# Relative-bias tables by one-hot products on TensorE, and the early projections as three rounded products with ScalarE rounding and GpSimd subtracting

## What is computed

```python
# first block, twice (DEPTH = 2)
h = layernorm(x)
proj = h @ w_in[layer]                       # -> aq ak av ag  bq bk bv bf bg  cq ck cv cg
oa = differential attention (4 heads, partial rope) * silu(ag)
ob = forgetting attention  (4 heads, cumulated log gates) * silu(bg)
oc = stick-breaking attention (4 heads) * silu(cg)
h = layernorm(ALPHA * h + concat(oa, ob, oc) @ w_out[layer])

# second block, once
h = rms_norm(x); proj = h @ w_in_2
score = sum over 8 index heads of relu(iq . ik) * iw ; sel = top_k(score, 128)
bias  = rel_bias[t5_bucket(pos[q] - pos[k])]          # 32 buckets, 4 heads
o_a = softmax(q . k_sel * scale + bias) @ v_sel       # 4 heads
o_b = gated linear recurrence in chunks of 64         # 4 heads
o_c = latent attention with its own low-rank q and kv # 4 heads
mixed = sum of sigmoid(gates) * (o @ w_up)            # three branches
x = x + mixed @ w_out_2
x = x + (silu(h @ w_gate) * (h @ w_up)) @ w_down      # h = rms_norm(x), D_FF = 2816
return rms_norm(x)
```

## Time and profile before

| | |
|---|---|
| runs, us | 2116.68, 2116.22, 2117.9; median 2116.68 |
| profiled execution: span from first to last instruction | 2112.8 us |
| median less the span | 3.9 us |
| mean granted TensorE clock | 0.942 of full speed |
| TensorE / VectorE / ScalarE / GpSimd busy | 90% / 54% / 32% / 1% |

### The profile page before, as it was taken

How to read it: one execution, slowest core, us unless ns; L and a number is a source line. 1 busy time by engine, 2 the same in 40 slices (tenths; PEclk the granted TensorE clock), 3 DMA queues, 4 the chain that set the end, 5 groups by cost and what they waited for, 6 DMA issues and landing times.

```text
span 2112.8 us, 19184 instructions
## 1 busy us (share of the span) xinstructions
PE 1902.5 (90%) x6900; PEld 1142.6 (54%) x6900; DVE 1142.6 (54%) x2306; ACT 667.5 (32%) x1340; POOL 25.4 (1%) x50
## 2 busy tenths in 40 slices
PE   5999999889899998989998876868999979999997
PEld 2444444434434444445333453556777868888785
DVE  4376676731999888532862352464445444444412
ACT  1123235311132344112112232335455334434411
POOL 2000000000000000000000000000000000000000
PEclk9999999999999998999998978978999979999998
DMA  6121112021211110032302011002333313332220
GB/s 219 40 80 40 41 49 67 27 80 40 80 40 40 40 70 1 1 111 72 89 20 60 12 59 30 14 18 75 90 90 102 113 41 99 100 98 84 98 100 40
DMA packets 153006, 135.79 MB, mean 64 GB/s; under 512 B 12673, under 2 KB 126977, under 8 KB 152913
## 3 DMA queue, kind: packets, MB, share of 16 engines
q1 hardware_dynamic: 149504, 124.53, 19.4%
q0 software_dynamic: 3408, 10.04, 1.6%
HBM read 130.36 MB, written 4.19 MB: 64 GB/s over the span
## 4 chain that ended last, share of the span: by engine, by line
PE 74%; DVE 16%; ACT 6%; issue 3%; DMA 1%; SPq 0%; DVEq 0%; ACTq 0%
PE proj L1262 24%; PE proj L1242 21%; PE proj L1259 11%; DVE rel_bias L1881 3%; PE proj L1239 2%; PE attn_out L1415 2%; PE score L1435 2%; PE score L1372 2%; PE proj L1435 1%; PE attn_out L1435 1%; PE turned_probs L1401 1%; DVE E L1951 1%; PE proj L1268 1%; PE turned_probs L1435 1%; DVE index_and_shared L1874 1%
## 5 line engine op out<-in xcount | busy, mean ns | idle before, releaser
L1262 PE MATMUL proj<-hT,weights 128*128 128x512 f32 x1216 | 561.9, 614 | 20.5 <-DVE raw L2135 11.4
L1262 PEld LDWEIGHTS proj<-hT,weights 128*128 128x128 f32 x1216 | 232.1, 196 | 302.6 <-issue 278.3
L1881 DVE SCALAR_TENSOR_TENSOR rel_bias<-index_and_shared,bias_deltas,rel_bias 128x128 f32<-128x128 f32 (+3 forms) x480 | 232.7, 547 | 4.3
L1242 PE MATMUL proj<-hT_high,weights_high 128*128 128x512 f32 x544 | 218.6, 402 | 7.6 <-DVE hT_low L2160 6.0
L1242 PE MATMUL proj<-hT_high,weights_low 128*128 128x512 f32 x544 | 215.8, 397 | 0.0
L1242 PE MATMUL proj<-hT_low,weights_high 128*128 128x512 f32 x544 | 215.5, 396 | 0.0
L2151 DVE TENSOR_TENSOR weights_low<-weights,weights_high 128x1024 fp32r<-128x1024 f32 (+1 forms) x122 | 135.3, 1116 | 96.4 <-ACT weights_high L1705 96.4
L1259 PE MATMUL proj<-weights,hT 128*128 128x512 f32 (+1 forms) x384 | 151.7, 553 | 0.1
L1705 ACT ACTIVATE weights_high<-weights 128x1024 fp32r<-128x1024 f32 (+1 forms) x122 | 111.5, 961 | 74.3 <-DMA weights<-in_w_ffn_down 60.5
L1242 PEld LDWEIGHTS proj<-hT_high,weights_high 128*128 128x128 f32 x544 | 103.2, 190 | 41.5 <-issue 9.5
L1453 ACT ACTIVATE tg<-proj 128x512 f32<-128x512 f32 x66 | 39.5, 599 | 267.0 <-PE proj L1242 212.2
(11 more groups left out here) (388 smaller groups left out, 2567.3 us busy)
## 6 DMA issues: line engine op xcount, KB each, us to landing
weights<-in_w_in SPq DMA_DIRECT2D x15, 2048.0 KB, 8.5
weights<-in_w_in SPq DMA_DIRECT2D x38, 512.0 KB, 4.2
weights<-in_w_ffn_gate SPq DMA_DIRECT2D x22, 512.0 KB, 4.1
weights<-in_w_ffn_up SPq DMA_DIRECT2D x22, 512.0 KB, 5.3
weights<-in_w_ffn_down SPq DMA_DIRECT2D x11, 1024.0 KB, 4.9
weights<-in_w_in SPq DMA_DIRECT2D x9, 1024.0 KB, 5.8
weights<-in_w_out SPq DMA_DIRECT2D x4, 2048.0 KB, 10.7
weights<-in_w_out SPq DMA_DIRECT2D x4, 1024.0 KB, 5.1
```

What stands on the lines that cost most here:

```text
L1242: mm = nc.tensor.matmul(ps[:, :], w_[:, k, c0:c0 + P], x_[:, k, :], start=first, stop=last)
L1262: mm = nc.tensor.matmul(ps[0:gr["M"], :], w[:, k, c0:c0 + gr["M"]], x[:, k, :], start=first, stop=last)
L1881: ins = nc.vector.scalar_tensor_tensor(o, mk, d, o, ALU.mult, ALU.add)
```

## The change

It does four things.

1. **Bias tables.** The 124 `bias` steps go. A small product (`bias_table`) makes, for each head, a row of 256 values indexed by 127 - residue; GpSimd stores it to DRAM and loads it back with one row shift for each partition (`circulant`). For each head a group `bias_rows` multiplies it by a one-hot matrix of the positions' residues modulo 128, and a group `bias` for each query tile multiplies the result by the keys' one-hot matrix. ScalarE copies both out. VectorE writes the two ends (keys ahead; keys 128 or more behind) over it with two `copy_predicated`. Two tables are made at each tick, in the first layer.
2. **Early projections.** All projections of stages 1 to 4, save the latents' second ones (`qb`, `kvb`), are made by three rounded products. `hT` is made as `hT_high` and `hT_low` at once by each `to_hT`; `y` is split in eight steps before `wo`.
3. **Weights.** Slabs of 128 columns (one piece of 8 x 128) for F groups and "wide" slabs of 512 columns in four pieces for T groups; a ring of 6 raw slots and one of 4 high slots in the first block, 4 and 2 in the second's woven stage, 9 and 9 in the tail. Everywhere, the tail too, ScalarE rounds and GpSimd subtracts in place. `place_splits` sets where in the list each piece's `split` stands.
4. **Order.** `wo` is done half 0 for all four tiles, then half 1 tile by tile with the layernorms; the last tile's transposes stand after the next stage's first two T groups; `wo2` has two wide slabs in place of four of 256 columns; `hi` is projected earlier.

In the diff `sp` is SyncE, `pool` GpSimd, `pe` TensorE, `act` ScalarE and `dve` VectorE.

```diff
-BIAS_RATES = {"A": 2.1, "B": 1.0, "C": 0.75}
+RAW_RING, HIGH_RING = [SLOT * i for i in range(6)], [SLOT * i for i in range(6, 10)]
+RAW_RING_2, HIGH_RING_2 = RAW_RING[0:4], [SLOT * 8, SLOT * 9]
+RAW_TAIL, HIGH_TAIL = [PIECE * i for i in range(TAIL_RING)], [PIECE * (TAIL_RING + i) for i in range(TAIL_RING)]
...
+    def slab(name, K=KD, cols=P, wide=False, split=True, **kw):
+        raws, highs = state["rings"]
+        n = 4 if wide else 1
...
+            at = state[ring]
+            if at + n > len(on):
+                at = 0
+            sl[ring] = on[at]
+            state[ring] = (at + n) % len(on)
...
-        while state["bias_due"] >= 1:
-            state["bias_due"] -= 1
-            if state["bias"] < len(bias_steps) and not only_block1:
-                steps.append(("bias", bias_steps[state["bias"]]))
+        for _ in range(2):
+            if state["bias"] < len(tables) and not only_block1:
+                h, t = tables[state["bias"]]
+                if t == 0:
+                    state["shifted"] = group("bias_rows", head=h)
+                g = group("bias", head=h, tile=t, rows=state["shifted"])
+                steps.append(("bias_ends", g))
                 state["bias"] += 1
...
+        for c in range(6):
+            steps.append(("split_x", ("y", c, 1)))
+        wo = slab("wo", wide=True, cols=512, layer=l, half=0)
...
+        wide_tiles(wo, (2, 3), dst=("resid", 0), src="y", layer=l)
+        wo = slab("wo", wide=True, cols=512, layer=l, half=1)
         for t in range(NT):
+            wide_tiles(wo, (t,), dst=("resid", 1), src="y", layer=l)
             steps.append(("ln", (l, t)))
...
+def place_splits(steps, groups, slabs, pieces):
...
+        seq = max(p["free_high"], min(p["free_raw"] + 2, slabs[p["slab"]]["first"] - 2))
+        k = max(at.get(seq, -1), start[p["after"]], before)
+        while steps[k + 1][0] not in ("group", "half", "down"):
+            k += 1
...
+            for p in pieces:
+                consumed(sp, p["free_raw"])
+                for dst, src in piece_loads(p):
+                    sp.dma_start(dst, src).then_inc(p["loaded"], 16)
...
+                elif op == "layer" and not only_block1:
+                    pool.wait_ge(table_stored, 16)
+                    pool.dma_start(circulant, table_back).then_inc(table_loaded, 16)
+                elif op == "split":
+                    p = pieces[arg]
+                    pool.wait_ge(w_high, p["nth"])
+                    nc.gpsimd.tensor_tensor(piece_view(WR, p, "raw"), piece_view(W, p, "raw"),
+                                            piece_view(WR, p, "high"), ALU.subtract).then_inc(w_low, 1)
...
+            def arrived(q):
+                    if p["split"]:
+                        pe.wait_ge(w_low, p["nth"])
...
                 elif op == "split":
+                    p = pieces[arg]
+                    act.wait_ge(p["loaded"], p["landed"])
+                    consumed(act, p["free_high"])
+                    nc.scalar.activation(piece_view(WR, p, "high"), piece_view(W, p, "raw"), ACT.Copy).then_inc(w_high, 1)
...
-                elif op == "split":
-                    i, q, n = arg["slab"], arg["piece"], arg["cols"]
-                    nc.vector.tensor_tensor(half_slots(WL, slabs[i])[:, r], half_slots(W, slabs[i])[:, r],
-                                            half_slots(WH, slabs[i])[:, r], ALU.subtract).then_inc(w_low, 1)
```

More of the change, by code:

```diff
@@ L430, in plan @@
             steps.append(("norm", dict(tile=NT - 1, nth=NT - 1)))
-        for t in ((NT - 2, NT - 1) if final_layer else (NT - 1,)):
-            for half in range(2):
-                group("to_hT", tile=t, half=half, layer=l, **(dict(norm=t) if final_layer else {}))
+            turn_rows(NT - 2, layer=l, norm=NT - 2)
     if not only_block1:
-        second(steps, groups, slabs, items, units, state, slab, group, weave, flush)
-    annotate(steps, groups, items, units)
-    return dict(steps=steps, groups=groups, slabs=slabs, items=items, units=units)
@@ L442, in second @@
+def second(steps, groups, slabs, items, units, state, slab, used, group, turn_rows, wide_tiles, weave, flush):
     l = DEPTH
@@ L444, in second @@
     steps.append(("angles", 0))
-    state["slots"] = [0, 1]
-    s_iq = slab("iq", K=KD, cols=512)
-    s_ak = slab("avak", K=KD, cols=392)
+    s_av = slab("avw", cols=136)
+    for t in range(NT):
+        if t == 2:
+            turn_rows(NT - 1, layer=DEPTH - 1, norm=NT - 1)
+        group("T", s_av, N=136, K=KD, tile=t, dst=("av", 0))
     for c in range(4):
-        group("F", s_iq, c0=128 * c, M=P, K=KD, dst=("qk", 4 + c), scale=1.0)
+        group("F", slab("iq", c0=128 * c), K=KD, dst=("qk", 4 + c), scale=1.0)
@@ new lines, in second, with values_hi, from_rest, latents_q @@
+    hold, rot = {}, {}
+    def values_hi(t):
+        if t == 0:
+            hold["hi"] = slab("hi", wide=True, cols=512)
+        group("T", hold["hi"], N=512, K=KD, tile=t, dst=("V", 512))
+    def from_rest(name, c, dst):
+        return group("F", slab(name, c0=128 * c), K=KD, dst=dst, scale=1.0)
+    def latents_q(c):
+        if c == 0:
+            state["rings"], state["raw"], state["high"] = (RAW_RING_2, HIGH_RING_2), 0, 0
+        from_rest("mq", c, ("cq", c))
+    def kpe():
+        rot["kpe"] = from_rest("mpe", 0, ("raw", 0))
@@ L557, in hgrn_gate @@
     def hgrn_gate(h):
-        g = group("gate", hold["last_hgrn"] if h < 3 else hold["hgrn"], c0=256, M=P, K=KD, chunk=4 + h, layer=l,
-                  first=False, unit=None)
+        g = group("gate", slab("hgrn", c0=HG + 128 * h), K=KD, chunk=4 + h, layer=l, first=False, unit=None)
         steps.append(("gate2", g))
@@ L616, in second @@
     steps.append(("split_x", ("mix", 7, 1)))
-    wo = tail[24:28]
-    for quarter in range(4):
-        last = quarter == 3
+    for half in range(2):
+        wo = slab("wo2", wide=True, cols=512, half=half)
+        last = half == 1
         for t in range(NT + last):
             if t < NT:
-                group("T", wo[quarter], c0=0, N=256, K=KD, tile=t, dst=("resid2", quarter), src="mix", parts=True)
-                if t in (1, 2):
-                    split_weights()
+                wide_tiles(wo, (t,), dst=("resid2", half), src="mix")
             if last:
@@ L645, in second @@
             steps.append(("split_x", ("act", c, 1)))
-        steps.append(("down", dict(i=i, slab=tail[28 + KF + i])))
-        split_weights(2)
+        two = [slab("down", K=1, cols=1024, at=2 * i + k) for k in range(2)]
+        for sl in two:
+            used(sl, len(groups) + i)
+        steps.append(("down", dict(i=i, slabs=two)))
     for t in range(NT):
```

718 lines of the change are left out of this document (359 added, 359 removed).

## The result

The changed kernel takes 2146.57 us (median of 4, 2146.41 to 2148.73); the kernel before, run beside it, 2116.52. The ratio is 1.0142, 95% interval 1.013 to 1.0154: 1.4% slower, where 2000 us and 5.5% faster were forecast. The profiled execution has a span of 2146.9 us.

What follows compares the result with a forecast made beforehand. The prediction took TensorE, busy 90% of the span, as the bound, then places where VectorE holds it up. Its terms summed to -117 us: span 2112.8 to 1996, with 3.9 us around it 2000 us; range 1945 to 2070.

Steps and rivals of the forecast that it cites:

- TensorE's gain: Projections, index phase and recurrence: 114 groups fall from 6.87 to 5.6 us as rounded products, -145 us.
- The four groups of 136 columns: Narrow groups, 7.4 us together before: 12 us as short rounded matmuls, bounds 7 to 21, so +5.
- VectorE's relief of 41 us: Both woven stages with drains: removing VectorE's bias steps gives -13 and -28 us, together -41, bounds 0 and -75.
- the drain: End of the first layer's woven stage: 12 to 14 attention items at 9 to 10 us each, -13 us.
- The tables at 12 us: First layer: four row groups of 0.86 us and 16 table groups, 8.6 us, on TensorE, +12.
- GpSimd's 2.4 us a piece: Weight slabs: a GpSimd subtraction takes 2.4 us, twice VectorE's, leaving TensorE to set the steady state.
- the coupling: GpSimd against VectorE's own steps: +5 us for an effect the trace can't show, bounds 0 and 50.
- rival 2: GpSimd and VectorE hold each other up on two-SBUF-input steps: 35 to 55 us more, 2045 us; chance 22%.
- wo to wo: Between wo's halves: the second half's slab loads late, leaving an 11 us hole in two layers, +22.
- hidden in the steady state: ScalarE's extra 115 rounded pieces, 120 us over 1440 us at a third of its load, cost nothing there.
- The recurrence: Recurrence stage: 12 of the 114 groups changing form, each falling from 6.87 to 5.6 us.
- Rival 4: Front held by chains, not TensorE: rounded products gain nothing, only the tables' relief counts, 2133 us; chance 3%.

Runs made afterwards that it cites:

- e14: The changed kernel without the table groups and without GpSimd's subtractions (third product takes the rounded weights): 2041.56 us, ratio 0.9639 to the kernel before.
- e1: The changed kernel with the 20 table groups left out and a VectorE fill of zeros for the predicated copies: 2106.57 us, ratio 0.9951 to the kernel before.
- e13: The changed kernel with VectorE's old bias steps in place of the tables, and without GpSimd's subtractions: 2086.11 us, ratio 0.985 to the kernel before.
- e15: The kernel before with the bias tables alone, fp32 projections kept and no GpSimd arithmetic: 2119.91 us, ratio 1.0017 to the kernel before.
- e5: The changed kernel with all 20 table groups in one block ahead of layer 0's first woven job: 2127.68 us, ratio 1.0054 to the kernel before.
- e3: The changed kernel with the weight subtractions on VectorE instead of GpSimd, at the same places: 2179.42 us, ratio 1.0292 to the kernel before.
- e8: The changed kernel with wo's second half multiplied by the first half's slab in both layers: 2121.47 us, ratio 1.002 to the kernel before.
- e17: The changed kernel with one wo slab for both halves, both halves of a tile multiplied one after the other: 2128.43 us, ratio 1.0051 to the kernel before.
- e18: A 2088.63 us version (GpSimd rounding narrow slabs, tables in a block, VectorE subtracting wo and av) with wo's second half one tile ahead of the layernorms: 2089.12 us.

## Why the prediction was wrong

The miss is 147 us. By medians it falls into three parts: with neither tables nor GpSimd (e14) the kernel takes 2041.6, where the sum without its 12 us for tables stood at 1988: 54 (at least, since the 1988 still hold what the sum had put down for GpSimd). GpSimd adds 2106.6 - 2041.6 = 65 (e1 against e14). The tables add 40 (the changed kernel against e1) where 12 were counted: 28.

1. **TensorE's gain: right.** The forecast was -145 + 5 - 3 = -143, the tables apart. In e14 TensorE's busy time is 1754.6 us, 148 less than before. In the tail and the woven stages a group of 24 takes about 5.5 us at full clock. The four groups of 136 columns took 21 us, the upper bound, where 12 were taken: they ran at the lower clock. The tail was right within 5 us: 7 us were gained in the feed-forward, and the stretch of wo2 came out 4 us longer where 3 less were forecast.

2. **VectorE's relief of 41 us on top of that: the first step that failed.** In layer 1's stage (F1 to L1) the sum had 29 groups x 1.27 = 37 us and 27 of relief beside them. The stage of e14 is 43 us shorter. TensorE's busy time in it fell by 44 (303.6 to 259.3), and its idle time, which the relief was to take away, stayed (15 before, 16 in e14). So the stage gained what TensorE's work and its clock (0.95 to 0.96) gave, and no more. The relief was not without worth: e14 is 44.6 us faster than e13, 34 of them in this stage. But the two gains are not separate terms. The rounded products alone (e13, without GpSimd as e14) took 9 us off the stage, the relief alone 15 (e15, which has its tables in the other layer), both together 43, and not 37 + 27. In layer 0 the 13 us of relief were put in the drain. In e15 the drain's last attention product ends 31.2 us behind L0, in the kernel before 36.2, so that some 5 of them were there. In e14 it ends 40.0 us behind L0, the gain being lost in a hole that the sum did not have (5).

3. **The tables at 12 us: the second.** I priced them as TensorE's work, which came to 16 us, and looked for no queue. Each group is read out by ScalarE and holds one of two banks, so a projection behind it waits for ScalarE's queue (the chain of the first ticks), and after the waits the products run at a lower clock (e1). Price 40 us woven, 19 less in a block (e5), and a 29 us longer stage even in the old kernel (e15). What stands queued behind a wait that the change adds was asked of the slabs, and not of the tables.

4. **GpSimd's 2.4 us a piece was right (2.5), its effect was not.** I gave the coupling 5 us and rival 2 a chance of 22%. Rival 2's mechanism is shown: VectorE's steps are lengthened by 96 us in all (858.6 against 762.2). It put 220 us there and took 16 to 25% of it as visible, 35 to 55; the lengthening was less, and the cost of GpSimd's part as a whole, duration and hold together, 65 to 71 us. How it divides between the two was not separated: e3 takes both away and puts a queue in their place.

5. **The holes: one was missing, and so was a wait.** wo to wo was forecast as 11 us a layer, which e8 bears out (11 and 15). But the list has no hole ahead of wo's first half, and there is one in each layer, 10.3 us long (7.9 in e14, where it waits for ScalarE). The load of the half's first piece is issued only when the last woven projection ends, at 393.6, and takes 3.9 us. Its rounding then stands behind six steps of splitting `y` in ScalarE's queue:

```profile
398.94 3.22 ACT hT_high L1774 x6
402.15 0.96 ACT weights_rounded L1758
403.18 2.37 POOL weights_rounded L1240
405.63 4.62 PE proj L1294 x12
```

The holes of the two layers are 20.6 of the 34.8 us that L1294 waits for GpSimd. The low halves of the turned rows were counted as VectorE's work alone; at the two boundaries TensorE waits 11.4 and 11.9 us for them, and 11.6 more for its transposes at the second, where it waited 7.5 in all for ScalarE's `hT` before. So the first boundary, L0 to F1, is 20 us longer than before: TensorE's busy time fell by 8.5 us (112.9 to 104.4, at a clock of 0.83 where it was 0.93; 12 cheaper groups were to give 15), and its idle time rose by 29. Putting groups elsewhere among the layernorms did not change that (e17, e18). The prediction called ScalarE's roundings hidden in the steady state; in the chain of the changed kernel one stands behind an item that top-k has held up, and TensorE's group behind both:

```profile
1098.57 0.76 DVE z L1990
1099.85 1.06 ACT weights_rounded L1758
1100.98 2.36 POOL weights_rounded L1240
1103.47 8.16 PE proj L1298 x24
```

6. **The recurrence** was forecast at -13 and came at -12 (latents to tail). Rival 4, that the front is held by chains, came nearest to the measured time (2133). That is luck in the number: TensorE's gain was there, and was spent again on waits that rival 4 does not name.

## What to carry to other kernels

A gain on the engine that is 95% busy and a relief of its helper are not two terms to add: in layer 1's stage one alone gave 9 us, the other alone 15, both 43, where the sum had 64. Forecast the busy engine's time with both, and ask of its idle time by itself who will still hold it up. Work moved "to the idle engine" has three prices beyond its duration: a place in the in-order queue of whoever reads it out, the bank it holds, and, between GpSimd and VectorE, the steps with two SBUF inputs. Ask of every read-out that the change adds in whose queue it stands and which bank it holds: the tables and the low halves of the turned rows cost TensorE waits of this kind. Where two changes came together, build the four combinations (here 2117, 2120, 2208 and 2147 us): the tables are worth nothing alone, and 62 us beside the rounded products.

## What the hardware showed beyond expectation

- A VectorE step of 512 columns with two SBUF inputs took up to 2.8 us beside a GpSimd subtraction that itself takes 2.35, against 0.69 alone; the mean of the 16 `qk` steps was 1844 ns. ScalarE's roundings kept their 1050 ns.
- GpSimd's one-input copy to fp32r, 1095 ns for 1024 columns, costs no more than ScalarE's, its two-input subtraction (2509 ns) twice VectorE's 1222.
- The four groups of 136 moving columns ran wholly at the lower clock (granted 0.50), 0.215 to 0.219 us a matmul; 256 columns took 0.21 at that clock. There about half the columns gave no shorter matmul.
